# RWKV front as one stage: low-rank products first, preparation passes between weight parts, gate product in the output stage

## What is computed

```python
xm = x[None] + (x_prev - x)[None] * mu[:, None, None, :]
rkv = jnp.einsum('pbtc,pcd->pbtd', xm[:3], w_rkv)
r, k, v = rkv[0], rkv[1], rkv[2]
w_log = -jax.nn.softplus(-(w0 + jnp.tanh(xm[3] @ w1) @ w2)) - 0.5
decay = jnp.exp(-jnp.exp(w_log.astype(F32)))
...
    v = v + (v_first - v) * jax.nn.sigmoid(v0 + (xm[2] @ v1) @ v2)
a = jax.nn.sigmoid(a0 + (xm[4] @ a1) @ a2)
g = jax.nn.sigmoid(xm[5] @ g1) @ g2
kk = (k * k_k).reshape(hd).astype(F32)
kk = kk / jnp.maximum(jnp.linalg.norm(kk, axis=-1, keepdims=True), 1e-12)
k = k * (1.0 + (a - 1.0) * k_a)
...
S, y = lax.scan(_wkv_step, wkv.astype(F32), seq)
...
y = y + jnp.sum(rh * kh * r_k, axis=-1, keepdims=True) * vh
out = (y.reshape(b, t, c).astype(x.dtype) * g) @ w_o
```

## Time and profile before

| | |
|---|---|
| median of 3 runs | 2838.97 us (2837.62 to 2840.88) |
| profiled execution: its own time | 2840.28 us |
| profiled execution: span, first to last instruction | 2838.5 us |
| mean granted TensorE clock | 0.905 |
| busy TensorE | 2490.6 us (88%) |
| busy VectorE | 1510.9 us (53%) |
| busy ScalarE | 1055.3 us (37%) |
| busy POOL | 194.6 us (7%) |
| HBM over the span | 96 GB/s |

### The profile page before, as it was taken

How to read it: one execution, slowest core, us unless ns; L and a number is a source line. 1 busy time by engine, 2 the same in 40 slices (tenths; PEclk the granted TensorE clock), 3 DMA queues, 4 the chain that set the end, 5 groups by cost and what they waited for, 6 DMA issues and landing times. The chain is left out here.

```text
span 2838.5 us, 48908 instructions
## 1 busy us (share of the span) xinstructions
PE 2490.6 (88%) x21191; PEld 2211.0 (78%) x21191; DVE 1510.9 (53%) x2378; ACT 1055.3 (37%) x1792; POOL 194.6 (7%) x197
## 2 busy tenths in 40 slices
PE   6968979998777999899999987589997985988999
PEld 5828959998545777789989956179997945968998
DVE  5456455534233777755434936365536537546643
ACT  3442224433313444444334631044433452324432
POOL 0030030000010000000000123400000002021000
PEclk8979979999967999999999966589998997978999
DMA  4210013434102122124433410524432410012442
GB/s 166 104 45 33 7 61 139 156 139 175 50 0 75 38 75 75 38 104 153 150 132 134 149 64 16 207 89 141 156 141 100 148 45 31 4 50 91 156 150 99
DMA packets 44422, 275.74 MB, mean 97 GB/s; under 512 B 5249, under 2 KB 5281, under 8 KB 14129
## 3 DMA queue, kind: packets, MB, share of 16 engines
q1 hardware_dynamic: 43968, 271.98, 27.0%
q0 software_dynamic: 240, 0.64, 0.1%
HBM read 256.36 MB, written 16.24 MB: 96 GB/s over the span
## 5 line engine op out<-in xcount | busy, mean ns | idle before, releaser
L337 PE MATMUL banks<-rounded,rounded 128*128 128x320 f32 x3184 | 1006.2, 316 | 90.0 <-DVE rounded L353 50.4
L338 PE MATMUL banks<-rounded,rounded 128*128 128x320 f32 x3184 | 991.6, 311 | 0.0
L339 PE MATMUL banks<-rounded,rounded 128*128 128x320 f32 x3184 | 990.9, 311 | 0.0
L327 DVE TENSOR_TENSOR rounded<-weight_ring,rounded 128x1024 fp32r<-128x1024 f32 x398 | 487.5, 1228 | 512.0 <-ACT rounded L320 511.7
L337 PEld LDWEIGHTS banks<-rounded,rounded 128*128 128x128 f32 x3184 | 605.4, 190 | 104.1 <-DVE rounded L353 55.5
L338 PEld LDWEIGHTS banks<-rounded,rounded 128*128 128x128 f32 x3184 | 605.6, 190 | 3.8
L339 PEld LDWEIGHTS banks<-rounded,rounded 128*128 128x128 f32 x3184 | 605.2, 190 | 0.0
L320 ACT ACTIVATE rounded<-weight_ring 128x1024 fp32r<-128x1024 f32 x398 | 420.4, 1059 | 406.8 <-PE banks L339 380.5
L1026 PE MATMUL banks<-arena 64*64 64x64 f32 x4032 | 139.6, 222 | 24.5 <-PEq L873 22.0
L1026 PEld LDWEIGHTS banks<-arena 64*64 64x64 f32 x4032 | 129.4, 137 | 30.9 <-issue 28.7
L522 ACT ACTIVATE arena<-banks 128x320 f32<-128x320 f32 x128 | 56.0, 437 | 233.4 <-PE banks L339 233.4
(11 more groups left out here) (377 smaller groups left out, 3043.2 us busy)
## 6 DMA issues: line engine op xcount, KB each, us to landing
weight_ring<-in_panels SPq DMA_DIRECT2D x206, 1024.0 KB, 4.7
arena<-in_pages SPq DMA_DIRECT2D x64, 320.0 KB, 3.4
arena<-in_ssm SPq DMA_DIRECT2D x8, 1024.0 KB, 7.7
out_ssm_sample<-arena SPq DMA_DIRECT2D x8, 1024.0 KB, 5.3
arena<-in_wkv SPq DMA_DIRECT2D x2, 2048.0 KB, 8.6
out_wkv_sample<-arena SPq DMA_DIRECT2D x4, 1024.0 KB, 3.8
consts<-in_consts SPq DMA_DIRECT2D x1, 1704.5 KB, 9.9
residual<-in_x SPq DMA_DIRECT2D x1, 1280.0 KB, 5.8
```

The costliest lines, as they stand in the source:

```text
L327: self.k.nc.vector.tensor_tensor(self.k.w_lo[:, i % SPLIT], self.raw(i), self.k.w_hi[:, i % SPLIT].bitcast(F32), ALU.subtract)\
L337: mm(out, hi, x_hi, start=start, stop=False)
L338: mm(out, hi, x_lo, start=False, stop=False)
L339: return mm(out, lo, x_hi, start=False, stop=stop)
```

## The change

`stage_rwkv_project` and `stage_rwkv_prepare` become one stage, `stage_rwkv_front`. TensorE's plan there begins with the low-rank inputs: decay and a as a pair of 64-column halves (hwa), the gate (hg, hb; in layer 3 hv beside hb), then LW and A in turn (rows 0 to 63, rows 64 to 127), in layer 3 SG. Then come the parts of K, R, V. The preparation's products stand between them: norm after R1, spread after R3 and R5, bonus after V5 and V7. VectorE makes the passes behind the `lo` of each part by a table (`extra`). ScalarE rounds the mixes and first weight parts between the low-rank evacuations, squares K from PSUM, and takes Exp after R1, Sqrt after R2, Exp after R4; in layer 0 it evacuates V twice (V and v_first), in layer 3 VectorE evacuates V. POOL has no pass left there. The hatted a uses the running sum's exponential shifted by one column, so the separate "before" sum and its exponential go; the first columns of each chunk are saved and put back.

The gate's second product is made in the output stage, between mean and variance. The panels are packed in the new order, the low-rank ones first; layer 3 has a panel of its own for v1 and v2, and the gate's second panel lies ahead of w_o. In Mamba the 32 heads' decay arrays are repeated on all 128 partitions, and the seg products alternate between rows 0 to 31 and 32 to 63, with outputs in other banks (4 to 7).

Core of the diff (pieces; the new stage in the main):

```diff
-PANELS = 4 * PANELS_FFN + 2 * PANELS_RWKV + PANELS_MLA + PANELS_MAMBA
+PANELS = 4 * PANELS_FFN + 2 * PANELS_RWKV + 1 + PANELS_MLA + PANELS_MAMBA
...
-def stage_rwkv_project(k, l, j):
+def stage_rwkv_front(k, l, j):
...
-    plan = [("R", m) for m in range(KT)] + [("K", m) for m in range(KT)] + [("V", m) for m in range(KT)]
+    plan = [("hwa", 0), ("hg", 0), ("hb", 0)]
+    for m in range(KT):
+        plan += [("LW", m), ("A", m)]
     if res:
-        plan += [("hv", 0)] + [("SG", m) for m in range(KT)]
-    plan += [("hw", 0)] + [("LW", m) for m in range(KT)]
-    plan += [("ha", 0)] + [("A", m) for m in range(KT)]
-    plan += [("hg", 0), ("hb", 0)] + [("G", m) for m in range(KT)]
+        plan += [("SG", m) for m in range(KT)]
+    first = len(plan)
+    plan += [(what, m) for what in "KRV" for m in range(KT)]
...
+            for i in range(KT):
+                mix(3, i)
+                mix(4, i)
+            for p in (5, 2, 1):
+                for i in range(KT):
+                    mix(p, i)
+            rest(1)
             split.lo(vec, 0)
+            split.lo(vec, 1)
+            vec.wait_ge(*pe_did.at("tile", tile["hwa", 0]))
+            for i in range(KT):
+                mix(0, i)
+            split.lo(vec, 2)
+            rest(0)
...
+            extra = {0: [lambda: running(4)], 8: [lambda: rest(2)], 10: [clamp], 11: [inverse],
+                     12: [lambda: unit(0)], 13: [lambda: unit(4), a_first], 14: [b_part], 15: [a_part, a_reset, key],
+                     16: [lambda: hats(0)], 17: [lambda: hats(1)], 18: [lambda: hats(2), lambda: value(0)],
+                     19: [lambda: hats(3), lambda: value(1)], 20: [lambda: value(2), bonus_in], 21: [lambda: value(3)],
+                     22: [lambda: value(4), lambda: bonus_out(0), lambda: bonus_out(1)],
+                     23: [lambda: value(5), lambda: bonus_out(2), lambda: bonus_out(3), lambda: value(6), lambda: value(7)]}
+            if res:
+                extra[2], extra[3] = [gate_first], [gate_own]
+            running(0)
             for n in range(24):
                 split.lo(vec, n + SPLIT)
...
+                for step in extra.get(n, ()):
+                    step()
+            vec.wait_ge(*pe_did.at("tile", tile["V", KT - 1]))
+            v.tensor_tensor(AR[:, :, CK:P], c3(R), c3(P_), ALU.mult).then_inc(*vec_did.tick("r_hat"))
+            for i in range(4, KT):
+                bonus_out(i)
...
+            after = {("R", 1): [norm], ("R", 3): [lambda: spread(0)], ("R", 5): [lambda: spread(4)],
+                     ("V", 5): [lambda: bonus(0)], ("V", 7): [lambda: bonus(4)]}
...
+                if what == "LW" and m == 0:
+                    round_mix(1)
+                    split.hi(act, 0)
+                    split.hi(act, 1)
+                if n == first:
+                    split.hi(act, 2)
+                    round_mix(0)
...
+                elif what == "K":
+                    if m == 0:
+                        act.wait_ge(*vec_did.at("cum", 3))
+                    if m == 4:
+                        act.wait_ge(*vec_did.at("cum", 7))
+                    s.activation(LW[:, m, :], b, ACT.Square, scale=k.param(f"k_k{j}", m)).then_inc(*act_did.tick("sq", m))
+                    s.activation(K[:, m, :], b, ACT.Copy).then_inc(*act_did.tick("tile", n))
...
             for i in range(KT):
                 nc.tensor.matmul(k.bank(i, T), k.const("mean64"), Y[:, i, :], start=True, stop=True).then_inc(*pe_did.tick("mean", i))
+            k.wait_panel(pe, lc)
+            for i in range(KT):
+                if i % 4 == 0:
+                    pe.wait_ge(*vec_did.at("centred", i // 4))
+                nc.tensor.matmul(k.bank(i, T), k.tile(lc, i), hg, start=True, stop=False)
+                nc.tensor.matmul(k.bank(i, T), k.tile(lc, 8 + i)[0:32, :], hb[0:32, :], start=False, stop=True)\
+                    .then_inc(*pe_did.tick("gate", i, also=[("panel", lc)] if i == KT - 1 else []))
             for i in range(KT):
                 pe.wait_ge(*act_did.at("sq", i // 4))
+                if i == 0:
+                    pe.wait_ge(*act_did.at("gate", 0))
...
                 def seg(q):
+                    if q == 0:
+                        pe.wait_ge(*act_did.at("bt", c))
+                        pe.wait_ge(*vec_did.at("cb", c))
                     if q >= 2:
                         pe.wait_ge(*vec_did.at("seg", c, q - 2))
                     for i in range(4):
-                        h = 4 * q + i
-                        ins = mm(k.ps[0:n, 6 + q % 2, i * P:i * P + n], k.const("ident")[0:MH, h:h + 1].to_broadcast([MH, n]),
-                                 AC[:, tok], start=True, stop=True)
+                        r = slice(MH * (i % 2), MH * (i % 2) + MH)
+                        h = MH * (i % 2) + 4 * q + i
+                        ins = mm(k.ps[0:n, 4 + q % 2 * 2 + i % 2, i // 2 * P:i // 2 * P + n], k.const("ident", r)[:, h:h + 1].to_broadcast([MH, n]),
+                                 AC[r, tok], start=True, stop=True)
```

More of the change, by code:

```diff
@@ L758, in _, with norm, spread @@
         @block.tensor
         def _(pe):
+            mm = nc.tensor.matmul
+            def norm():
+                for i in range(KT):
+                    pe.wait_ge(*act_did.at("sq", i))
+                    ins = mm(k.bank(4, T)[0:16, :], head_mean(k, 64, i), LW[:, i, :], start=i == 0, stop=i == KT - 1)
+                ins.then_inc(*pe_did.tick("norm"))
+            def spread(m0):
+                pe.wait_ge(*vec_did.at("inv"))
+                for i in range(m0, m0 + 4):
+                    if i >= 4:
+                        pe.wait_ge(*vec_did.at("kk", i - 4))
+                    head_spread(k, 64, i, k.bank(4 + i % 4, T), inv).then_inc(*pe_did.tick("spread", i))
@@ L767, in _ @@
                     for i in range(KT):
                         if m == 0:
[L769 to L778, removed]
-                            if i == 0:
-                                k.wait_panel(pe, lb)
-                            o, lhs = out[32:64, :], k.tile(lb, i)[:, 32:64]
-                        elif what == "hw":
-                            if i == 0:
-                                k.wait_panel(pe, la)
-                            o, lhs = out[0:64, :], k.tile(la, i)[:, 0:64]
-                        elif what == "ha":
-                            o, lhs = out[64:128, :], k.tile(la, i)[:, 64:128]
-                        elif what == "hg":
-                            o, lhs = out, k.tile(la, 8 + i)
-                        else:
-                            o, lhs = out[0:32, :], k.tile(lb, i)[:, 0:32]
-                        ins = nc.tensor.matmul(o, lhs, src[:, i, :], start=i == 0, stop=i == KT - 1)
-                    ins.then_inc(*pe_did.tick("tile", n))
-                    continue
@@ L923, in _ @@
+                            pe.wait_ge(*vec_did.at("mix_lo", p, i))
+                        ins = split.product(out, w, i, hi[p][:, i, :], lo[p][:, i, :], i == 0, i == KT - 1)
+                    also = [("part", w)]
+                ins.then_inc(*pe_did.tick("tile", n, also=also))
+                for step in after.get((what, m), ()):
+                    step()
         @block.scalar
@@ L941, in _ @@
[L941 to L958 removed]
+            s.activation(rs, k.bank(7, T), ACT.Sqrt, bias=k.eps(0)).then_inc(*act_did.tick("root"))
@@ L1346, in _ @@
                 nc.scalar.activation(SQ[:, fs, :], Y[:, fs, :], ACT.Square).then_inc(*act_did.tick("sq", g))
+            for i in range(KT):
+                act.wait_ge(*pe_did.at("gate", i))
+                nc.scalar.activation(G[:, i, :], k.bank(i, T), ACT.Copy).then_inc(*act_did.tick("gate", i))
             split.hi(act, 1)
```

473 lines of the change are left out of this document (238 added, 235 removed).

## The result

The changed kernel takes 2776.08 us, the median of 4 runs (2773.36 to 2778.55), beside 2839.19 for the kernel before: a ratio of 0.9778, with a 95% interval of 0.9765 to 0.979, 63 us less. The forecast was 2776, within 2746 to 2808. The profiled execution took 2774.72 with a span of 2772.9, against 2840.28 and 2838.5. K0 is the first weight part of K, R3 the fourth of R, and so on.

A forecast was written before the change was run, and what follows sets the result against it. It took two successive phases, each idling one engine, as the bound. Fronts -34.8 and -39.8, output +22.0 and Mamba -10.5 sum to -63.1: the profiled 2840.28 becomes 2777.2, median 2776 us, range 2746 to 2808.

The forecast's parts named there:

- front, layer 0: Layer 0 from the norm's root to the first scan product: 201.8 us to fall to 167.0, by 34.8.
- output, two stages: Gate products between mean and variance add 11.0 us a stage, +22.0 in all; bounds 8 and 20 a stage.
- Mamba: Scan's segment products side by side on two row groups, 2.00 to 1.05 us a step: -10.5, bounds 0 and -13.
- The walk of TensorE's queue: Front of layer 0, priced entry by entry with its waits: first scan product at 187.3 us instead of 222.15.
- The sign of more than 25 us of idle TensorE: In the front, TensorE idle for more than 25 us would show the forecast wrong.
- The clock: Front: TensorE restarts at half clock after thin outputs and waits, costing 2.4 us each time, first at K0.
- Layer 3's values: Layer 3's front: two VectorE passes of 0.5 us per V part, where VectorE is late, add 1.5.
- The new wait: Mamba: wait for B's copy at a chunk's head, 0.8 us, hidden behind POOL's mask; uncovered 2.4 in all.
- The slower rival: Wide VectorE passes in both fronts take 8.19 us even without POOL, 86 more in all: 2862; chance 0.03.
- The rival of passes that hide better: TensorE's front waits and two clock losses, 19.5 us a stage, go: half gone 2756, all 2737; chance 0.14.
- What the first part says of the bound: Low-rank products and preparation stand behind each other, one engine idling in each; the change lays preparation passes between weight parts.
- The tables: ScalarE's Exp, Sqrt, Exp order: a table load costs 1.28 us; the skill's 2.66 would add 2.8 in sum.

The follow-up runs named there:

- e2: Changed kernel with Mamba's segment products all on rows 0 to 31 again, without pairs on two row groups: 2788.72 us.
- e3: Changed kernel with three wide POOL passes of unused result added in layer 0, from the unit key on: 2787.09 us.
- e7: Changed kernel with a new order: norm, root, reciprocal, second spread, (a-1)k, b, a, key and first roundings earlier, bonus later: 2740.65 us.
- e5: Changed kernel with the first spread moved from behind R3 to behind R4: 2767.58 us.
- e6: Changed kernel with (a-1)k made behind the rest of part 12 and part 19 rounded before ScalarE evacuates V0: 2770.88 us.
- e1: Changed kernel with all passes from the spread on moved behind V7, no longer hidden beside weight parts: 2782.17 us.
- e9: Kernel before the change, with only POOL's three preparation passes moved to VectorE: 2828.83 us against 2839.03.

## Why the prediction was right

The time came out to the microsecond, in part by luck: the terms were off by up to 2.2 us, in both directions, and the profiled executions differ by 65.6 where the medians differ by 63.1.

| term | forecast | measured |
|---|---|---|
| front, layer 0 | -34.8 | -36.5 |
| front, layer 3 | -39.8 | -39.0 |
| output, two stages | +22.0 | +19.8 |
| Mamba | -10.5 | -9.3 |

- *The walk of TensorE's queue* held. K0 was put at 41 us after the root and came at 39.5; waits of 6.3, 5.4 and 3.0 came as 4.78, 5.29 and 3.82 at the three places named. Rest plus hat came every 3.9 on VectorE (rests at 155.46 and 159.34) where 4.0 was put, but did not pace V4 and V5: V3 had run in part at half clock, and they followed without a wait.
- *A sign of the forecast failed.* VectorE was to be over 80% busy from K0 to V7. By the stretches it was busy for 73.75 of the 117.3 us from K0 to V6, 63%, and for 3.28 of the 14.90 with the wait, the spread and R4. The sign of more than 25 us of idle TensorE did not say from where it counts: by the same rows it is 23.0 from the first low-rank product on, and near 34 from the root.
- *The clock* was half right. The loss at K0 (2.4) was not there: granted 1.00 from 59.3 to 108.9. It lay in the low-rank part instead (0.83), behind the wait of 4.38, and was over before K0. The losses after the waits are there, at the spread more than was put: 2.2 on its 8 products (4.53 instead of 2.37) and about 2 on R4, where 2.4 was put in all.
- *Layer 3's values* were mis-sized: the term was +1.5 on VectorE, the trace has 7.25 of waiting at V4, partly in place of layer 0's longer waits (V3 3.36 instead of 5.29, the bonus 0.28 instead of 3.82). The stage came out right by that trade.
- *Mamba*: a step fell to 1.16 (1657.01 - 1655.85), not 1.05, so the pairs are not quite side by side; 0.84 a step instead of 0.95. The new wait is at the chunks' heads and hidden as said (the first y product comes no later), but it is for VectorE's `cb`, not for B's copy, and longer than 0.8 (1.74 in a long chunk); uncovered, bounded at 2.4, it goes with 2.9 in e2.
- *Output*: the gates took the 11.6 of the earlier trace rows; in layer 0 the mean ran at full clock (4.54 against 6.2 before), which returned 1.7.
- *The slower rival* had 0.03 and its price is real: 7 us a pass beside POOL (e3). What excludes it is the empty POOL, and L891 had the right price, if only because it began ahead of POOL.
- *The rival of passes that hide better* had 0.14. Its prices hold in sum: twice 19.5 was put for waits and clock, and with nearly all of them gone e7's fronts are 40.0 shorter, at 2740.65 where 2737 was worked out. What spoke against it was "its queue is in order, and from R4 on it holds as much work as TensorE". For the order as changed that held: the waits came. As a bound it did not: VectorE was busy for 63% of the time, and in e7 the same work fits into layer 0 without a wait, from K0 on, once the norm, the reciprocal, the second spread, (a-1)k, the key and some roundings stand earlier and the bonus later. The bound was the place of a few entries in the queue; e5 and e6 show two of them, the rest moved together.
- *What the first part says of the bound* needs a correction too: it puts the gain down to two phases laid over each other. e1 shows that of the front's 36.5 in layer 0 hiding the wide passes gave 5.5: they spare 35 us behind V7 (5 instead of 40), and V7 itself ends at 180 instead of 150, with 13.9 us of waits, 10.5 of spreads and bonus products, and lost clock ahead of it. Of the rest, 11.6 are gates that moved to the output stage, 10.9 the preparation's head between the parts, 5.4 the earlier start with pairs, and 3.1 the passes with POOL empty (4.6 by e9, on the old order); these are read from marks, not tried one by one. The forecast's total was right, since it walked TensorE's queue with these waits in it.
- *The tables*: one load shows 1.28 here too, begins 0.01 after the rounding ahead of it (124.19, 1.06 long), and Exp begins 0.01 after it, so the 2.66 for a switch that the Trainium skill gives ("ScalarE: Activation LUTs", "What ACT_TABLE_LOAD costs") is not seen as a gap in this trace.

```profile
125.26 1.28 ACT L1008 ACT_TABLE_LOAD   x1
126.55 2.34 ACT L1008 ACTIVATE arena<-arena 128x2560 f32<-128x2560 f32 x1
```

## What to carry to other kernels

Work that is moved beside a full engine is worth its length less the waits it brings to that engine, so put the serial version with the cheap passes on the same sheet: here the overlap gave 5 us out of 40 until its order was mended. Walk each in-order queue and ask of every wait which entry stands ahead of the awaited one without need; moving one spread by one part gave 6.0 and 7.5 us a layer. A coming-out total proves little: compare the terms stage by stage.

## What was not expected of the hardware

- A small VectorE pass waits whole for POOL: in e3 a scalar pass of 64 elements with one input, 0.25 us in the changed kernel, took 4.50 when POOL's first pass had begun 0.06 before it, and ended 0.10 after that pass. POOL waits in turn: its three equal passes took 4.47, 5.46 and 6.91, the third with a whole VectorE pass (L798, done at 145.23) ahead of it.
- The granted clock was down to a mean of 0.83 over the low-rank part, where the forecast put no loss, and full for all of K0 to R3 behind it, where it put one. It was at half speed twice there: in the first 3 us or so, behind 12.39 of idle, and for about 4.5 from 52.95 on, behind the wait of 4.38.
- Four 32-row products take 1.16 in pairs on two row groups and 2.00 one after another: a factor of 1.7, not 2.
